# Two expert streams woven into each other on TensorE, over one ring of raw buffers

## The reference

```python
def _swiglu(x, w_gate, w_up, w_down):
    return (jax.nn.silu(x @ w_gate) * (x @ w_up)) @ w_down

logits = (x @ w_router)                      # 8 experts
top_v, top_i = lax.top_k(logits, 2)
gates = jax.nn.softmax(top_v, axis=-1)
combine = sum(one_hot(top_i, 8) * gates[..., None], axis=1)
for e in range(8):
    out = out + combine[:, e:e+1] * _swiglu(x, w_gate[e], w_up[e], w_down[e])
```

## Time and profile before

| | |
|---|---|
| median of three runs | 1328.16 us |
| profiled execution | 1328.74 us, span 1326.8 us |
| TensorE (PE) busy | 1304.6 us, 98% |
| PE weight loads | 983.3 us, 74% |
| VectorE (DVE) busy | 795.7 us, 60% |
| ScalarE (ACT) busy | 642.6 us, 48% |
| read from HBM | 423.16 MB, 320 GB/s over the span |
| expert stage | from about 480 us to the end |

### The profile page before, as it was taken

How to read it: one execution, slowest core, us unless ns; L and a number is a source line. 1 busy time by engine, 2 the same in 40 slices (tenths; PEclk the granted TensorE clock), 3 DMA queues, 4 the chain that set the end, 5 groups by cost and what they waited for, 6 DMA issues and landing times.

```text
span 1326.8 us, 18843 instructions
## 1 busy us (share of the span) xinstructions
PE 1304.6 (98%) x7654; PEld 983.3 (74%) x7654; DVE 795.7 (60%) x957; ACT 642.6 (48%) x672; POOL 4.5 (0%) x12
## 2 busy tenths in 40 slices
PE   9999999999999999999999999999999999999996
PEld 8999999999999977884448885347887345888332
DVE  7564765653888679972129884118885215888122
ACT  6655644352576587761027772017774005776001
POOL 0000000000000000000000000000000000000000
PEclk9999999999999999999999999999999999999998
DMA  7335354463333499999999999999999999999995
GB/s 299 136 128 190 127 191 159 159 220 140 115 143 128 169 377 341 348 376 405 409 411 426 428 427 426 427 399 426 426 427 427 427 405 427 427 427 426 427 426 227
DMA packets 72347, 425.50 MB, mean 321 GB/s; under 512 B 6384, under 2 KB 8432, under 8 KB 27328
## 3 DMA queue, kind: packets, MB, share of 16 engines
q1 hardware_dynamic: 71680, 422.67, 78.7%
q0 software_dynamic: 432, 1.54, 0.3%
q10 hardware_dynamic: 144, 0.02, 0.0%
HBM read 423.16 MB, written 1.05 MB: 320 GB/s over the span
## 4 chain that ended last, share of the span: by engine, by line
PE 84%; DVE 9%; ACT 3%; issue 3%; DMA 1%; SPq 0%; DVEq 0%; ACTq 0%
PE ps L2388 14%; PE ps L2259 7%; PE ps L2260 7%; PE ps L2265 7%; PE ps L2419 7%; PE ps L1720 5%; PE ps L1710 4%; PE ps L1711 4%; PE ps L2284 4%; PE ps L2285 4%; PE ps L2292 4%; PE ps L1758 2%; PE ps L1775 2%; PE ps L1759 2%; DVE wl L1173 1%
## 5 line engine op out<-in xcount | busy, mean ns | idle before, releaser
L1383 DVE TENSOR_TENSOR wl<-raw,wh 128x2048 fp32r<-128x2048 f32 x96 | 218.6, 2289 | 23.9 <-ACT wh L855 23.8
L855 ACT CAST wh<-raw 128x2048 fp32r<-128x2048 f32 x96 | 183.9, 1916 | 66.8 <-PE ps L2260 40.3
L2259 PE MATMUL ps<-wh,gh 128*128 128x512 f32 x448 | 175.3, 391 | 0.7 <-DVE gl L1457 0.7
L2260 PE MATMUL ps<-wh,gl 128*128 128x512 f32 x448 | 174.4, 389 | 0.0
L918 ACT ACTIVATE sil<-ps 64x512 f32<-64x512 f32 x28 | 16.5, 589 | 299.2 <-PE ps L2390 299.2
L2388 PE MATMUL ps<-raw,few 128*64 128x512 f32 x288 | 130.2, 597 | 0.6 <-DMA raw<-in_moe_w_up 0.6
L2390 PE MATMUL ps<-raw,few 128*64 128x512 f32 x288 | 129.5, 597 | 0.0
L2265 PE MATMUL ps<-wl,gh 128*128 128x512 f32 x448 | 119.8, 389 | 0.0
L1596 DVE COPY few_act<-ps 128x256 f32<-128x256 f32 x28 | 11.9, 425 | 177.9 <-PE ps L2402 177.9
L1047 DVE TENSOR_TENSOR wl<-raw,wh 128x4096 fp32r<-128x4096 f32 (+1 forms) x18 | 73.2, 4069 | 61.7 <-ACT wh L614 39.7
L614 ACT CAST wh<-raw 128x4096 fp32r<-128x4096 f32 (+2 forms) x29 | 92.0, 3173 | 34.5 <-PE ps L1711 34.1
(11 more groups left out here) (343 smaller groups left out, 2692.0 us busy)
## 6 DMA issues: line engine op xcount, KB each, us to landing
raw<-in_moe_w_up SPq DMA_DIRECT2D x71, 1024.0 KB, 12.1
raw<-in_moe_w_gate SPq DMA_DIRECT2D x70, 1024.0 KB, 12.1
raw<-in_moe_w_down SPq DMA_DIRECT2D x51, 1024.0 KB, 13.6
unsplit<-in_moe_w_down SPq DMA_DIRECT2D x33, 1024.0 KB, 10.6
unsplit<-in_moe_w_up SPq DMA_DIRECT2D x25, 1024.0 KB, 14.2
unsplit<-in_moe_w_gate SPq DMA_DIRECT2D x22, 1024.0 KB, 17.3
raw_more<-in_moe_w_down SPq DMA_DIRECT2D x15, 1024.0 KB, 11.6
raw<-in_diff_w_qkv SPq DMA_DIRECT2D x8, 1536.0 KB, 6.6
```

Of the source, the lines that this page charges most:

```text
L855: act.copy(split_piece(wh, p), raw_piece(p, first)).then_inc(wh_ready, 1)
L1383: dve.tensor_tensor(split_piece(wl, p), raw_piece(p, first), raw_f(split_piece(wh, p)), ALU.subtract).then_inc(wl_ready, 1)
L2259: pe.matmul(ps[:, bank, :], gh[:, s], w, start=(k0 + k == 0), stop=False)
L2260: ins = pe.matmul(ps[:, bank, :], gl[:, s], w, start=False, stop=False)
```

## The change

Wide and few units become two streams of 28 chunks (`CHUNKS`) each, and one loop runs over both, the few stream two chunks behind (`LAG`). All pieces, 168 of either stream (`STREAM`), are put into one order that follows the loop, with wide pieces moved forward by three places (`AHEAD`), and take the eleven raw slots in turn. The six borrowed slots go. In the order the first few piece is number 13 (counted from 0), so SyncE's wait for `routed` now stands ahead of number 13. The few stream gets its own SiLU and product tiles and its own PSUM banks (5 and 6). `few` has two halves. Gathers for the next pair come in four parts of 128 + 64 columns at once; scatters come one bank at a time, all through PSUM bank 7; a few unit's output is scattered as a high and a low half stacked in the 128 rows, in fp32r. `sort_experts` now runs before the splits of pieces 1 and 2, `count_units` and `list_units` in step 0, `pick_pair(0)` in step 1.

The core of the diff; the loops of TensorE and VectorE are cut to what sets the order:

```diff
-WIDE_PLACES = places(((8, 9, 10, *range(8)), ROUND, range(10), range(10)))
-FIRST_PLACES = places((ROUND, ROUND, range(10), range(10)))
-FEW_PLACES = places(((10, *range(10), *range(RAW_SLOTS, RAW_SLOTS + LENT)), range(9), range(8), range(8)))
+CHUNKS = WIDE_UNITS * FC
+LAG, AHEAD = 2, 3
+        def piece_order():
+            order, few_from = [], []
+            for s in range(CHUNKS + LAG + 1):
+                t = s - LAG
...
+                for a, b in ((0, 2), (2, 4), (4, 5), (5, 6)):
+                    order += [("wide", p) for p in wide[a:b] if p is not None]
+                    order += [("few", p) for p in few[a:b] if p is not None]
+            sooner = sorted(range(len(order)), key=lambda n: n - AHEAD * (order[n][0] == "wide"))
+            return [order[n] for n in sooner]
...
+            for q, (stream, p) in enumerate(pieces):
+                s = q % RAW_SLOTS
...
+                    held, of = pieces[q - RAW_SLOTS]
+                    if held == "wide":
+                        sp.wait_ge(wl_ready, C_MOE + of + 1)
+                    else:
+                        sp.wait_ge(few_used, of + 1)
...
+                    if unit == ("few", 0):
+                        sp.wait_ge(routed, 1)
...
+            def gather_part(n, q):
...
+                for k in range(2):
+                    for t in range(QT):
+                        ins = pe.matmul(ps[:, 7, k * WITH_FEW:(k + 1) * WITH_FEW], bm["tok"][:, t, (2 * q + k) * P:(2 * q + k + 1) * P],
+                                        bm["pick"][:, t, 0:WITH_FEW], start=(t == 0), stop=(t == QT - 1), skip_group_check=True)
...
+            def scatter_few(n, k, bank=7):
...
+                s, to = slice(k % 2 * BANK, (k % 2 + 1) * BANK), bm["payT"][:, SEQ + k // 2 * P:SEQ + (k // 2 + 1) * P]
+                pe.matmul(ps[:, bank, :], to, bm["y_few"][:, s], start=True, stop=True).then_inc(sc_done, 1)
...
+            for s in range(CHUNKS + LAG + 1):        # TensorE
+                t, n, r = s - LAG, s // FC, s % FC
...
+                    wide_up(s, "g")
...
+                    few_up(t, 0)
...
+                    few_turn(t - 1)
...
+                    wide_up(s, "u")
...
+                    few_up(t, 1)
+                if gathers:
+                    gather_part(n + 1, 0)
...
+                    wide_down(s - 1, 0)
+                if s < CHUNKS:
+                    wide_turn(s)
+                if gathers:
+                    gather_part(n + 1, 1)
...
+                    few_down(t - 1, 0)
...
+                    wide_down(s - 1, 1)
...
+                    few_down(t - 1, 1)
...
+                if s == 1:
+                    gather_few()
...
+            for s in range(CHUNKS + LAG + 1):        # VectorE
...
+                    split_if(g + 3)
+                    split_if(g + 4)
+                    if s < 2:
+                        save_tokens(2 + s)
+                    if s == 0:
+                        count_units()
...
+                    split_if(u + 3)
...
+                    dve.tensor_tensor(bm["act"][:], bm["sil"][:], ps[:, 1, :], ALU.mult).then_inc(eprod_ready, 1)
+                    split_if(u + 4)
+                    if s == 0:
+                        list_units()
...
+                if s == 1:
+                    dve.wait_ge(gathered, 2)
+                    pick_pair(0)
```

More of the change, by code:

```diff
@@ L409, in raw_place, with landing, landing_in, more_piece @@
                 return raw_more[:]
[L410 to L421, removed]
+            if s < 9:
+                return unsplit[:, s - 7, SPLIT_SLOTS // 2, SPLIT_SLOTS % 2 * PIECE:(SPLIT_SLOTS % 2 + 1) * PIECE]
+            return flat[:, 0:PIECE] if s == 9 else sq3[:]
+        def landing(kind, p):
+            return raw_place(position[kind, p] % RAW_SLOTS)
+        def landing_in(kind, p):
+            q = position[kind, p]
+            return piece_landed[q % RAW_SLOTS], 16 * (q // RAW_SLOTS + 1)
+        def more_piece(p):
+            return raw_place(MORE_PLACES[p][0])
+        def more_in(a, p):
+            s = MORE_PLACES[p][0]
+            times = sum(1 for at_ in MORE_PLACES if at_[0] == s)
+            so_far = sum(1 for q in range(len(pieces)) if q % RAW_SLOTS == s)
+            return piece_landed[s], 16 * (times * a + so_far - times * WIDE_UNITS + sum(1 for at_ in MORE_PLACES[:p + 1] if at_[0] == s))
         def last_at(taken, s):
@@ L434, in split_piece, with split_free @@
             return w[:, slot // 2, slot % 2 * PIECE:(slot % 2 + 1) * PIECE]
[L436 to L453, removed]
+        def split_free(p):
+            return C_MOE + (-1 if p == 0 else p + 1 - SPLIT_SLOTS)
         def landed(c):
@@ L875, in _, with gathered_high @@
                          ps[:, BACKS[n], :]).then_inc(back_ev, 1)
-            unit_split(0, 0, 1, first=True)
-            def gathered_high(k, halves=(0, 1)):
-                for h in halves:
+            split(1)
+            def gathered_high(k):
+                for h in range(2):
                     act.wait_ge(gathered, k * 2 + h - 1)
@@ new lines, in few_up @@
+            def few_up(c, half):
+                p, n = few_up_at(c) + 2 * half, c // FC
+                out_, few = ps[:, 5, :], bm["few"][:, n % 2]
+                if half == 0:
+                    pe.wait_ge(few_ready, 1 + PARTS * n)
+                    if c:
+                        pe.wait_ge(few_prod, c)
+                pe.wait_ge(*landing_in("few", p))
+                pe.wait_ge(*landing_in("few", p + 1))
+                for k in range(KD // 2):
+                    to = slice((half * (KD // 2) + k) * SMALL, (half * (KD // 2) + k + 1) * SMALL)
+                    s = slice(k * WIDE, (k + 1) * WIDE)
+                    first_, last_ = half == 0 and k == 0, half == 1 and k == KD // 2 - 1
+                    gate = pe.matmul(out_[0:SMALL, :], few[:, to], landing("few", p)[:, s], start=first_, stop=last_,
+                                     skip_group_check=True)
+                    up_ = pe.matmul(out_[SMALL:, :], few[:, to], landing("few", p + 1)[:, s], start=first_, stop=last_,
+                                    skip_group_check=True)
+                gate.then_inc(few_used, 1)
+                up_.then_inc(few_used, 1)
@@ L2244, in unit_body @@
+            for k in range(2 * QT):
+                scatter_few(FEW - 1, k, 2 + k)
+            def unit_body(u, a):
                 gh, gl = bm["gh"], bm["gl"]
@@ L2344, in unit_body @@
                         down(i - 1, (1,))
-                    if first and i == 5:
-                        gather_few(0)
-                        turn_picks(0)
-                    if scatter and i == 3:
+                    if i == 3:
                         pe.wait_ge(pick_ready, u + 1)
@@ L2450, in _ @@
[L2450 to L2454 removed]
+            pe.nop().then_inc(gathered, 2 * (WIDE_UNITS - 1))
+            pe.nop().then_inc(payT_done, E)
+            pe.nop().then_inc(half_done, E)
             pe.wait_ge(routed, 1)
```

781 lines of the change are left out of this document (454 added, 327 removed).

## The result

The changed kernel takes 1354.24 us (median of four runs, 1353.48 to 1357.56), the kernel before 1328.0 us (four runs, 1327.37 to 1329.48). The ratio is 1.0201, with a 95% interval of 1.0181 to 1.022: slower, by 26 us. The forecast was 1343 us with a range of 1320 to 1356. Direction and main cause held; 11 us of the loss were not in the sum, and 1354.24 lies just above the part of the range (1335 to 1354) that the sum stood for.

What follows compares the result with a forecast made beforehand. PE was taken to bound the expert stage, loads close behind. Steady state +8.6 (28.6 for changes less 20 saved), start +6.0 and end +0.6 gave +15.2 on 1328.7, 1343.9, forecast as 1343 us, range 1320 to 1356.

Steps and rivals of the forecast that it cites:

- the part of the range (1335 to 1354): Whole kernel: the forecast as worked out would land at 1335 to 1354 us, chance 0.58.
- What bounds: Expert stage: PE bounds it, with the loads 2.5 us a pair behind; after the change a pair still exceeds the loads' 206.3.
- Changing shapes: Woven steps on PE: 0.16 us wide to few, 0.22 few to wide; 26 steps at 1.1 give +28.6 us.
- The plain step: One woven step of the loop on PE: 28.9 us, against 27.8 before.
- The estimate by a drain: Woven steps: 0.16 us for each of eight changes and two turns of 0.35 give 28.6 us a step.
- Gathers and scatters: PE's work beside the chunks: merged gathers, scatters and boundaries fall from 52 to 32 us, saving 20 us.
- The start: PE waits 4.6 us for VectorE's first product and 3.3 for the picks; less 1.9, +6.0 us, bounds 0 and +12.
- The end: Last output: two 64-row copies and a subtraction replace one copy, with a shorter scatter; +0.6 us (0 to 2).
- Load-bound: Rival for the stage: frequent shape changes cost nothing, loads at 206.3 us a pair take over; 1313 us, chance 0.12.
- Same bound, nothing lost: Rival: PE still binds, with trips at half price or a start without stalls; 1328 to 1335 us, chance 0.17 for 1322 to 1335.
- Helpers late at the gathers: Rival at bank 7: gather parts wait for ScalarE and VectorE behind splits, +20 us, 1363 us; chance 0.13 for 1354 and above.

Runs made afterwards that it cites:

- a kernel of its own: Separate small kernel without loads: blocks of wide-type products and side-by-side pairs in turn, in several formats; 0.40 us there and back, 0.39 in longer blocks.
- two trips: Changed kernel with both start waits treated, PE going from wide to few stream and back twice a step instead of four times: 1339.19 us; six places ahead, 1333.94.
- one trip: Changed kernel with both start waits treated, PE going wide to few and back once a step: 1343.22 us; five ahead, copy before split, start reordered: 1330.56.
- the last kernel: Kernel going wide to few and back once a step, five places ahead, with units listed straight after counting and first pair picked earlier: 1324.71 us, ratio 0.9982.

## Why the prediction was right, and where it was short

**What bounds.** Right. PE was the bound before and after; the run without the stop of the loads, at 1354.27, leaves their idle time at the start no part in the loss.

**Changing shapes.** The main term, right in kind and nearly in size. The plain step was put at 28.9 and is 29.01 to 29.04 us. The 0.40 us for one change there and back, taken from one kind of row, held in three ways: in a kernel of its own (0.39 to 0.40), and in a pair where one change a step goes, with two trips (211.46 - 208.55 = 2.9, 0.42 a step) and again with one (2.7, 0.39). The 0.11 us a step that the sum lacked make 3 us over 26 steps; it is spread over turns and changes, and no row isolates it. The legs themselves were put a little too high where the way leads into few (0.16, measured 0.14). The estimate by a drain, 28.6, is further off.

**Gathers and scatters.** The pair was put at about 211 and is 211.46. A merged gather part takes 1.39 us to the next start, which is 5.6 a gather against 5.5 in the sum. Here luck had a part: 0.249 us scaled from 128 to 192 columns is 0.37 and not the 0.34 that the sum took, and the measured 0.35 lies close to a number that no row gave:

```profile
879.72 1.46 PE L2336 MATMUL ps<-pick,tok 128*128 128x192 f32 x8
881.11 1.94 PE L2492 MATMUL ps<-sq,few_act 128*64 128x512 f32 x8
```

With the steps, the steady part became 11.6 us longer, not 8.6. (PE's stage, from its first product to the end of the last few one, went from 832.3 to 857.0 us; less waits and clock, 24.7 - 6.4 - 6.7 = 11.6.)

**The start.** The two waits came where they were put, and for the reasons given in the main: 3.8 us for the product (put at 4.6) and 4.5 for the picks (put at 3.3), 8.3 against 7.9. In the second the sum left out what stands ahead of the split itself, ScalarE's cast of the same piece (to 514.97 us) and `eal` on VectorE (to 515.06), both of which end behind PE's last product (to 513.88). That the two errors nearly cancel is luck. The failing step is the sentence that follows, "Together 7.9, less the 1.9 that go: +6.0 us". It prices a wait on PE at its length, and puts the time behind it at nothing. Behind each wait PE ran at 1.2 GHz for some microseconds, and that cost 6.7 us more; moving the picks alone gave 9.2 us for a wait of 4.5, and moved the time from 1354.24 to 1345.08. This one term is two thirds of the difference between the profiled run, 1353.66, and the sum, 1343.9. The trace of before had no gap of that length in the stage, so its rows could not show it; with it the start cost 8.3 + 6.7 - 1.9 = 13.1 us more, above the prediction's bound of +12.

**The end.** Put at +0.6 (0 to 2), it is +1.1. The last scatter begins 2.13 us behind the end of the last few product, since a 64-row cast and a subtraction stand between, where it was 0.68; from its start to the end of the kernel it is 0.3 us less.

In sum: 11.6 + 6.4 + 6.7 + 1.1 = 25.8 us, less 0.8, since the stage's first product comes at 479.77 instead of 480.59 us. That is the 25.0 by which the span grew.

**The rivals.** Load-bound at 1313: false as stated, since changing shapes is not free. The bound itself is real: with one trip a step the loads do take over, though at 207.5 us a pair and not at 206.3. The 1313, and the 1315 to 1318 expected of one trip, were too low by that at least, 1.2 us a pair. Same bound, nothing lost, 1328 to 1335: the trips kept their full price, and treating the start alone left 1344 us. Helpers late at the gathers: no such wait in the trace, though the median falls into that rival's band (1354 and above). Yet the mechanism, a short piece of work queued behind a split, decided the one-trip kernel: 18.9 us, most of them gone by moving one copy.

## What to carry to other kernels

- Where a trace has an operation a few times, its price per use can hold when a loop makes it dense, as it did here: sum starts to starts, both legs, and multiply. Weaving two streams of different tile shapes on TensorE costs 0.4 us for each change there and back here, so make the blocks long rather than the interleaving fine: from four trips to one (four changes to two) gave 5.6 us a pair of PE's time. Together with the order on VectorE, the loads five ahead and the start, it turned the loss into a small gain.
- In a stage that runs densely at full clock, price a new wait of some microseconds above its length; here one of 4.5 us cost 9.2.
- In an in-order queue, put what TensorE waits for ahead of what waits for a landing; and in one ring for two consumers, loading one stream further ahead takes slots from the other (with one trip a step, eight places ahead took 56 us more than five; the order at the start differed too).

## What was not expected of the hardware

After waits of 3.8 and 4.5 us in an otherwise full stream the granted clock went to 0.50, and products started 0.43 instead of 0.227 us apart, for some 3 us behind the first wait and 10 behind the second. The Trainium skill, TensorE: Matmul & The Clock Gate, Part 1, knows these two levels; the rows agree. How short a wait does it is not settled: 2.7 us in one piece brought 0.83 over 10 us, and 1.5 and 1.1 us near each other still 0.84 over 20 us, while single ones of 1.8, 1.7, 1.4 and 0.8 us in the last kernel left it at 1.00.

The change of number format between fp32r and fp32 costs 0.02 us a trip, where the change of shape costs 0.37.
